# Suffix and chunk sums of a log decay: one plain fp32 matmul each, or a rounded part and a remainder

## The reference

```python
loga = jax.nn.log_sigmoid((a_lr @ w_gate_up + b_gate).astype(jnp.float32)) / GATE_TAU
loga = loga.reshape(B, nc, CHUNK, GLA_HEADS, GLA_DK)
cum = jnp.cumsum(loga, axis=2)
cum_end = cum[:, :, -1:]
k_dec = kc * jnp.exp(cum_end - cum)          # decayed keys
u_c = jnp.einsum('bnchk,bnchv->nbhkv', k_dec, vc)
a_c = jnp.moveaxis(jnp.exp(cum_end[:, :, 0]), 1, 0)
state = a[..., None] * state + u             # once per chunk, then o = q @ state
```

## Time and profile before

| | us |
|---|---|
| median of three runs | 1251.17 |
| the profiled execution's own time | 1251.65 |
| its span in the profile | 1249.9 |
| TensorE (PE) busy | 1239.3 |
| VectorE (DVE) busy | 792.1 |
| ScalarE (ACT) busy | 566.9 |
| GpSimd (POOL) busy | 240.3 |

### The profile page before, as it was taken

How to read it: one execution, slowest core, us unless ns; L and a number is a source line. 1 busy time by engine, 2 the same in 40 slices (tenths; PEclk the granted TensorE clock), 3 DMA queues, 4 the chain that set the end, 5 groups by cost and what they waited for, 6 DMA issues and landing times.

```text
span 1249.9 us, 17399 instructions
## 1 busy us (share of the span) xinstructions
PE 1239.3 (99%) x6456; PEld 1037.9 (83%) x6456; DVE 792.1 (63%) x1144; ACT 566.9 (45%) x1021; POOL 240.3 (19%) x362
## 2 busy tenths in 40 slices
PE   9999999999999999999999999999999999999998
PEld 8998987878888888888878888888888888888886
DVE  6862666467864653546886666767866756565646
ACT  6575546564433532435554333333333334545432
POOL 1323122040110200021200000013554545000003
PEclk9999999999999999999999999999999999999999
DMA  9989677574410211121223545556654557897723
GB/s 383 389 271 378 171 224 206 163 185 152 169 67 36 85 51 51 52 84 68 73 103 119 204 180 188 209 189 224 235 173 152 176 201 248 288 339 232 239 86 135
DMA packets 76340, 224.33 MB, mean 179 GB/s; under 512 B 9040, under 2 KB 9184, under 8 KB 76256
## 3 DMA queue, kind: packets, MB, share of 16 engines
q1 hardware_dynamic: 59040, 163.95, 37.6%
q0 software_dynamic: 15776, 54.03, 13.3%
q10 hardware_dynamic: 1440, 5.24, 1.0%
HBM read 171.80 MB, written 68.16 MB: 192 GB/s over the span
## 4 chain that ended last, share of the span: by engine, by line
PE 91%; DMA 4%; issue 2%; DVE 2%; ACT 1%; POOL 1%; DVEq 0%; ACTq 0%; POOLq 0%
PE ps L2065 30%; PE ps L2066 29%; PE ps L2067 29%; DMA block_su_t<-in_w_in 2%; PE ps L2096 1%; DMA raw<-in_w_xkv 1%; DMA raw<-in_w_in 1%; PE ps L2218 1%; ACT ps L1062 0%; DVE w_lo L644 0%; DMA mem_first<-in_mem_t 0%; POOL rstd L915 0%; PE ps L2125 0%; PE ps L2166 0%; ACT w_hi L635 0%
## 5 line engine op out<-in xcount | busy, mean ns | idle before, releaser
L2065 PE MATMUL ps<-w_hi,act_hi 128*128 128x512 f32 (+1 forms) x448 | 171.0, 382 | 0.0
L2067 PE MATMUL ps<-w_hi,act_lo 128*128 128x512 f32 (+1 forms) x448 | 167.9, 375 | 0.0
L2066 PE MATMUL ps<-w_lo,act_hi 128*128 128x512 f32 (+1 forms) x448 | 167.8, 375 | 0.0
L2066 PE MATMUL ps<-act_lo,w_hi 128*128 128x512 f32 x384 | 149.4, 389 | 0.0
L1801 DVE TENSOR_TENSOR w_lo<-wraw,w_hi 128x512 fp32r<-128x512 f32 x126 | 95.9, 765 | 74.2 <-ACT w_hi L1281 74.1
L2065 PE MATMUL ps<-sums_hi,w_hi 128*128 128x512 f32 x352 | 137.2, 390 | 0.8 <-issue 0.8
L2067 PE MATMUL ps<-sums_hi,w_lo 128*128 128x512 f32 x352 | 137.0, 389 | 0.0
L1281 ACT ACTIVATE w_hi<-wraw 128x512 fp32r<-128x512 f32 x126 | 78.6, 628 | 90.5 <-PE ps L2067 71.0
L2065 PE MATMUL ps<-act_hi,w_hi 128*128 128x512 f32 x296 | 115.4, 390 | 0.1
L2067 PE MATMUL ps<-act_hi,w_lo 128*128 128x512 f32 x296 | 115.2, 389 | 0.0
L1807 DVE TENSOR_TENSOR w_lo<-wraw,w_hi 128x1024 fp32r<-128x1024 f32 x53 | 69.1, 1305 | 57.5 <-ACT w_hi L1292 57.2
(11 more groups left out here) (313 smaller groups left out, 2622.6 us busy)
## 6 DMA issues: line engine op xcount, KB each, us to landing
wraw<-in_w_ffn_gu SPq DMA_DIRECT2D x42, 512.0 KB, 4.3
hidden_a<-ffn POOLq DMA_DIRECT2D x44, 256.0 KB, 3.4
hidden_s<-ffn POOLq DMA_DIRECT2D x44, 256.0 KB, 2.3
wraw<-hidden_s SPq DMA_DIRECT2D x35, 256.0 KB, 3.4
wraw<-down_sums SPq DMA_DIRECT2D x31, 256.0 KB, 4.5
wraw<-in_w_ffn_down SPq DMA_DIRECT2D x27, 256.0 KB, 4.4
b_raw<-in_w_in SPq DMA_DIRECT2D x12, 512.0 KB, 5.1
block_vg_t<-in_w_in POOLq DMA_DIRECT2D x6, 1024.0 KB, 9.0
```

The costliest lines, as they stand in the source:

```text
L2065: nc.tensor.matmul(out_, lh, rh, start=first, stop=False, skip_group_check=onto)
L2066: nc.tensor.matmul(out_, lh, rl, start=False, stop=False, skip_group_check=onto)
L2067: return nc.tensor.matmul(out_, ll, rh, start=False, stop=last, skip_group_check=onto)
```

## The change

The log decay is split as the other operands are. In the rows of `resid` a second view `log_parts` of type fp32r is placed. Once the log decay of a block stands, ACT writes its rounded part over min(z, 0), which is no longer needed (`log_hi`), and DVE writes the remainder over the log decay itself (`log_lo`). The suffix sum is then two fp32r matmuls with `later`, and each chunk sum two with `inchunk`; zeros and ones have no remainder. `later` and `inchunk` become fp32r, cast by POOL from float32 tiles in the last rows of `resid`.

`log_hi(t - 3)` and `log_lo(t - 3)` stand in the evacuation of step `k` t, ahead of the gate of block t - 2; those of blocks 5, 6 and 7 in the evacuation of the first three `p1` steps.

```diff
         resid = place("resid", [P, TT, D], F32, at["resid"])
+        log_parts = place("log_parts", [P, TT, D], F32R, at["resid"])
...
-        later = little("later", [P, P])
-        inchunk = little("inchunk", [P, 2])
+        later = little("later", [P, P], F32R)
+        inchunk = little("inchunk", [P, 2], F32R)
+        later_raw = place("later_raw", [P, P], F32, at["resid"] + 31 * K)
+        inchunk_raw = place("inchunk_raw", [P, 2], F32, at["resid"] + 31 * K + 512)
...
-            pool.memset(later[CHUNK:P, 0:CHUNK], 0.0).then_inc(consts, 1)
-            pool.memset(inchunk[0:CHUNK, 0:1], 1.0).then_inc(consts, 1)
-            pool.memset(inchunk[CHUNK:P, 1:2], 1.0).then_inc(consts, 1)
+            link(pool.memset(later_raw[CHUNK:P, 0:CHUNK], 0.0))
+            pool.memset(inchunk_raw[0:CHUNK, 0:1], 1.0).then_inc(consts, 1)
+            pool.memset(inchunk_raw[CHUNK:P, 1:2], 1.0).then_inc(consts, 1)
+            pool.wait_ge(consts, 3)
+            link(pool.tensor_copy(later[:, :], later_raw[:, :]))
+            pool.tensor_copy(inchunk[:, :], inchunk_raw[:, :]).then_inc(consts, 1)
...
+            def log_hi(t):
+                act.wait_ge(loga_ready, 2 * t + 1)
+                nc.scalar.activation(log_parts[:, t, KW:2 * KW], resid[:, t, 0:KW], ACT.Copy).then_inc(loga_hi, 1)
...
                     if t >= 2:
+                        if t >= 3:
+                            log_hi(t - 3)
                         gate(t - 2)
...
-                    if st == 0 and i < 2:
-                        gate(TT - 2 + i)
+                    if st == 0 and i < 3:
+                        log_hi(TT - 3 + i)
+                        if i < 2:
+                            gate(TT - 2 + i)
...
+            def log_lo(t):
+                dve.wait_ge(loga_hi, t + 1)
+                nc.vector.tensor_tensor(log_parts[:, t, 0:KW], resid[:, t, 0:KW],
+                                        log_parts[:, t, KW:2 * KW].bitcast(F32),
+                                        ALU.subtract).then_inc(loga_ready, 1)
...
                     if t:
                         gate_rows(t - 1)
+                    if t >= 3:
+                        log_lo(t - 3)
                     if t >= 2:
                         gate(t - 2)
...
+                        log_lo(TT - 3 + t)
                         gate(TT - 2 + t)
+                    elif kind == "vg" and b == 0 and t == 2:
+                        log_lo(TT - 1)
...
-                    dve.wait_ge(consts, 1)
+                    dve.wait_ge(consts, 4)
...
-                pe.wait_ge(loga_ready, t + 1)
+                pe.wait_ge(loga_ready, 2 * t + 2)
                 if t:
                     pe.wait_ge(suf_read, t)
-                lg = resid[:, t, 0:KW]
                 b = suf_psum(t)
-                nc.tensor.matmul(ps[:, b, 0:KW], later[:, :], lg, start=True, stop=True)
+                for o in (KW, 0):
+                    nc.tensor.matmul(ps[:, b, 0:KW], later[:, :], log_parts[:, t, o:o + KW],
+                                     start=o == KW, stop=o == 0)
                 for pr in range(2):
-                    ins = nc.tensor.matmul(ps[:, b, KW + 2 * pr:KW + 2 * pr + 2],
-                                           resid[:, t, pr * P:(pr + 1) * P], inchunk[:, :], start=True, stop=True)
+                    for o in (KW, 0):
+                        ins = nc.tensor.matmul(ps[:, b, KW + 2 * pr:KW + 2 * pr + 2],
+                                               log_parts[:, t, o + pr * P:o + (pr + 1) * P], inchunk[:, :],
+                                               start=o == KW, stop=o == 0)
```

More of the change, by code:

```diff
@@ L524, in build @@
         a_read, a_turned, a_ready = sem("a_read"), sem("a_turned"), sem("a_ready")
-        z_done, z_read, gate_e, gate_l, loga_ready = (sem("z_done"), sem("z_read"), sem("gate_e"),
-                                                      sem("gate_l"), sem("loga_ready"))
+        z_done, z_read, gate_e, gate_l, loga_ready, loga_hi = (sem("z_done"), sem("z_read"), sem("gate_e"),
+                                                      sem("gate_l"), sem("loga_ready"), sem("loga_hi"))
         suf_done, suf_read, kdec_ready = sem("suf_done"), sem("suf_read"), sem("kdec_ready")
@@ L870, in _ @@
             pool.memset(ident[:, :], 0.0).then_inc(pool_own, 1)
-            pool.memset(later[:, :], 1.0).then_inc(pool_own, 1)
-            pool.memset(inchunk[:, :], 0.0).then_inc(pool_own, 1)
+            pool.memset(later_raw[:, :], 1.0).then_inc(pool_own, 1)
+            pool.memset(inchunk_raw[:, :], 0.0).then_inc(pool_own, 1)
             pool.memset(mhalf[:, :], -0.5).then_inc(pool_own, 1)
@@ L878, in _ @@
                                base=0, pattern=[[-1, P]], channel_multiplier=1).then_inc(consts, 1)
-            link(pool.affine_select(out=later[:, :], in_=later[:, :], compare_op=ALU.is_gt, fill=0.0,
+            link(pool.affine_select(out=later_raw[:, :], in_=later_raw[:, :], compare_op=ALU.is_gt, fill=0.0,
                                     base=0, pattern=[[-1, P]], channel_multiplier=1))
-            pool.memset(later[CHUNK:P, 0:CHUNK], 0.0).then_inc(consts, 1)
-            pool.memset(inchunk[0:CHUNK, 0:1], 1.0).then_inc(consts, 1)
-            pool.memset(inchunk[CHUNK:P, 1:2], 1.0).then_inc(consts, 1)
+            link(pool.memset(later_raw[CHUNK:P, 0:CHUNK], 0.0))
[4 more added lines that the diff above has]
+            pool.tensor_copy(inchunk[:, :], inchunk_raw[:, :]).then_inc(consts, 1)
             pool.wait_ge(consts, 4)
```

## The result

| | before | after |
|---|---|---|
| median of 15 runs, us | 1251.31 | 1253.71 |
| lowest and highest | 1250.54, 1253.02 | 1253.06, 1254.61 |
| the profiled execution's own time | 1251.65 | 1253.06 |
| its span | 1249.9 | 1251.3 |

The ratio is 1.0019, with a 95% interval of 1.0012 to 1.0026: the change is 2.4 us slower. That is under 0.2% and too little for one run or a few to show, but clear over fifteen. The forecast was 1253.2 us, 2.0 to 2.1 above before, in a range of 1250.9 to 1254.6.

A forecast was written before the change was run, and what follows sets the result against it. TensorE bounds the kernel, and DVE and ACT work delays it: 2.7 us late at the first p2 product, less 0.6 from three cheaper suffixes, is +2.1, as a median 1253.2 us; range 1250.9 to 1254.6.

The forecast's parts named there:

- first p1 step: DVE's lag at the first p1 block: 0.57 us wait for ACT's copy plus 0.34 work, less 0.09 spare, giving 3.26.
- second p1 step: DVE's lag at the second p1 block: an old idle time of 1.47 us absorbs part, leaving 2.81.
- at 180 us: End of the changed stretch: TensorE 2.1 us late, 2.7 less 0.6 that the three remaining suffixes save.
- The lag: From the fourth k block on, DVE's queue falls behind by 0.34 us a subtraction plus waits for ACT's copy.
- The waits of TensorE: TensorE late by 1.16 us at block 5's gate, 2.0 and 2.5 at second and fourth suffixes, 2.7 at first p2.
- The first gap of 0.22 us: Before the change, TensorE's gate matmul starts 0.22 us after DVE's copy of aT ends: little slack.
- A suffix: TensorE's suffix step falls from 0.87 to 0.68 us (bounds 0.50 to 0.80), about 0.20 saved, eight times.
- The rule on passes: Fp32r halves passes on TensorE; if passes set time, the two-column step falls from 0.36 to 0.18 us; left open.
- The second rival: Two-column fp32r matmuls dearer (suffix 0.82 us or more) and lag full: +2.5 to +2.8 us; chance 0.26.
- The start: Kernel start: POOL's two more casts and DVE's wait for four constants instead of one cost nothing.
- Nothing is regained: After 180 us: the 0.4 us wait at 267.73 stays, since its transfer also starts 2.1 us later.
- The signature: Profile after, 126 to 180 us: TensorE busy time lower by some 1.6 us, idle time higher by some 3.7.

The follow-up runs named there:

- e3: The change with DVE's subtraction moved inside the gate chain, between -|z| and the log decay; 1250.52 us, ratio 0.9990.
- e2: The kernel before plus ACT's eight copies and DVE's eight subtractions, suffix left as plain float32 matmuls; 1254.56 us, ratio 1.0023.
- e1: The change without ACT's eight copies and DVE's eight subtractions, only the fp32r suffix step and its casts; 1250.22 us, ratio 0.9990.
- e4: Against e3, the last block's copy and subtraction one step later, behind the fourth b_lo; 1250.01 us, ratio 0.9986.
- e7: Against e4, each chunk sum from the rounded part alone, two matmuls of two columns a suffix instead of four; 1248.76 us, ratio 0.9976.
- e5: The change without DVE's eight subtractions, ACT's copies kept; 1250.46 us, ratio 0.9990.
- e6: The change without ACT's eight copies, DVE subtracting min(z, 0) instead of the rounded part; 1252.45 us, ratio 1.0006.

## Why the prediction was right

By its own steps, places counted as above (the 0.46 us of the earlier start added):

| step | forecast | measured |
|---|---|---|
| lag of DVE after k4 (min(z, 0)) | 1.05 | 1.05 |
| after k5, at aT of block 5 | 1.39 | 1.37 |
| after k7 | 2.44 | 2.42 |
| first p1 step | 3.26 | 3.02 |
| second p1 step | 2.81 | 2.93 |
| at the fourth b_lo | 3.15 | 3.24 |
| TensorE late at the gate of block 5 | 1.16 | 1.30 |
| at the second suffix | 2.0 | 2.11 |
| at the fourth suffix | 2.5 | 2.70 |
| in the first p2 product | 2.7 | 2.8 |
| at 180 us | 2.1 | 2.36 |

- **The lag.** Right in its mechanism and nearly its sizes; e3 shows it by taking the subtraction off the chain with nothing else changed. The wait for ACT in the k steps was 0.36 and 0.37 by the starts, as forecast. Mis-sized was the one in the first p1 step: 0.35, not 0.57. Before, ACT's evacuation of the p1 product starts 0.29 behind the decay (153.26, 153.55); on the late ACT it starts 0.05 behind it (155.23, 155.28), so the copy behind it comes 0.24 sooner, about what the forecast had too much. For the second p1 step the forecast gives 2.81 without its terms; the copy stands behind the evacuation of a product that TensorE itself now gives late, DVE waited 1.05 for it by the bracket, and the lag was 2.93. The two errors have opposite signs, and that the lag at the fourth b_lo came out so close (3.15, 3.24) owes something to luck.
- **The waits of TensorE.** Most came out 0.1 to 0.2 us longer than worked out. The forecast let TensorE go on sooner when released: from aT's start to the gate matmul it took 0.31, and 0.43 was measured (149.69 to 150.12); from the decay's start to the suffix 0.20, and 0.31 was measured (155.23 to 155.54). e2 too, without cheaper suffixes, is 3.08 at 180 where the same working gives 2.8. Of the 0.26 that the forecast is short at 180, 0.07 were there at the b_lo (2.77, not 2.7), 0.13 came right behind that wait, where the next matmul follows after 0.34 instead of 0.23 (169.77, 170.11), and 0.06 from suffixes that save 0.18 and not 0.20. In e1 and e4, where it does not wait, the working (-1.4) is off by 0.1.
- **Slips in the working.** The first gap of 0.22 us is at aT of block 5; the prediction calls it block 6 there and block 5 in its sum. That sum, 148.78 + 1.39 + 0.31, is 150.48 and so 1.20 late, not 1.16. The wait at the gate of block 4 was left out, though the lag of 1.05 at its aT gives one: its copy started at 144.68 before, and 144.68 + 1.05 + 0.31 is 0.27 behind 145.77, where the matmul started. Measured are 0.38. None of this moves the result, as the later waits are longer.
- **A suffix.** Forecast 0.68, by the period of the last ones (171.26 to 174.71, 3.45 less 12 x 0.23) 0.69. The 256 column pair took 0.23 (forecast 0.24), the four small ones 0.37 (0.36).
- **The rule on passes.** By the four passes of true FP32 (the Trainium skill, "FP8 and Floating Point Precision", TensorE Precision Notes) the two-column step would have halved to 0.18. It didn't: 0.36 before with eight passes by the rule, 0.37 after with four. For 256 columns the rule holds (0.43 to 0.23). What sets the pace of the small ones goes by records, and their number, four, stayed. Each of these records has a load of 128x128 weights beside it, since the log decay is the side that is loaded here (the row below). Whether the load or the matmul sets the pace was not tested.

```profile
174.83 0.53 PEld L2195 LDWEIGHTS ps<-inchunk,log_parts 128*128 128x128 f32 x4
```

- **The second rival** asked for a suffix of 0.82, or a lag at the fourth b_lo of about 3.0. The suffix was 0.69. The lag is not clearly worded: for DVE the forecast itself already had 3.15 there, so only TensorE's lateness can be meant, and that was 2.8. The rival's cause did not come, yet its size nearly did: +2.4 against its +2.5 to +2.8. The median of 1253.71 lies at the upper edge of the forecast's own 1252.4 to 1253.7.
- **The start.** The casts on POOL were put at nothing. The instruction of DVE behind the four constants starts at 28.36 instead of 28.27, and the ones ahead of it are 0.09 later too (26.89, 26.80), so it waited for nothing new.
- **Behind 180 us.** "Nothing is regained" is not what the profiles show at first sight: the wait of 0.42 us at 267.73 is missing after, and the spans differ by 1.4 where 2.36 less the 0.46 would be 1.9. The first transfer of that chain did start later as forecast, by 1.90 us (239.28 to 241.18). But from there to the b_lo that TensorE needs it took 27.18 us before and 26.70 after, a stretch of transfers that POOL issues and of the splits behind them.

Before:

```profile
266.46 1.22 DVE L1740 TENSOR_TENSOR b_lo<-b_raw,b_hi 128x1024 fp32r<-128x1024 f32 x1
```

After:

```profile
241.18 1.22 POOL L952 DMA_DIRECT2D block_su_t<-in_w_in  x1 [0.31 <-POOL rstd L921]
...
267.88 1.21 DVE L1765 TENSOR_TENSOR b_lo<-b_raw,b_hi 128x1024 fp32r<-128x1024 f32 x1
```

The same stretch took 26.44 us in e7, where the wait is missing too, and 27.71 in e5, where it is longest. In all seven profiles that have the wait, it is the stretch less 26.75 or 26.76 us, whatever the kernel and however late TensorE is: 0.42 before, and 0.18, 0.49, 0.17, 0.24, 0.96 and 0.38 in e1 to e6. So the wait comes from how long the transfers of that execution took, and the change regains nothing there. Why the transfers differ is not shown. The medians, over many executions, keep the full 2.4. The longest of these waits, in e5:

```profile
266.30 0.50 PE L2085 MATMUL ps<-b_hi,s_hi 128*128 128x512 f32 x1 [0.96 <-DVE b_lo L1760]
```

- **The signature.** Forecast were 3.7 us of new idle time and 1.6 less busy time. The records show 2.6 of idle in the windows and 0.4 less busy over the whole span. By the starts, the five waits cost 0.39, 0.84, 1.09, 0.89 and 0.40, together 3.6: a part of each wait is drawn as busy time, in longer rows (0.67 instead of 0.60 for the gate pair). The lateness at 180 is the safer measure.

## What to carry to other kernels

Extra work on an engine that is busy 63% of the time is free, as these runs show it, only where its queue is idle: look for the instruction that waits, here 0.93 us between -|z| and the log decay, and put the new one just ahead of it. The same instruction one place earlier, ahead of the chain, cost 3.3 us at 180 against the placement of e3 (2.36 later and 0.93 earlier than before), because there it delays what two other engines wait for, and waits itself for ACT's copy. To size such a change, carry a lag from step to step and compare it at each place with the slack of whoever waits there; lags at successive places are not summed.

## What the runs showed of the hardware that was not expected

With a load of 128x128 weights for each, a matmul of two columns costs nearly as much as one of 256: 0.09 us from start to start in a row of four, 0.11 saved for each that goes (e7), against 0.12 for fp32r at 256 columns. Its type made no difference here: four plain float32 records took 0.36 us and four of fp32r 0.37. The chunk sums of two columns make up over half of the suffix step after the change (0.37 of 0.69). Matmuls of two columns that keep their weights were not tried.
